# Forget-gate attention pairs: weights divided before the turn, values as 64-column stationary tiles, output written by feature

## The reference, cut to what matters

```python
s = einsum('bhqd,bhkd->bhqk', q, k) * scale + c[q] - c[k]     # c: cumulated log forget gate
p = softmax(where(causal, s, min))
fox_o = einsum('bhqk,bhkd->bhqd', p, v)                       # 8 heads x 64
diff_o = rms_norm(a1 - lam * a2, subln_g) * 0.8               # 4 heads x 128
m = concat([fox_o, diff_o]) @ w_out                           # 1024 x 1024
x = x + rms_norm(m, mix_post_g)
```

## Time and profile before

| what | value |
|---|---|
| median of 3 runs | 992.6 us |
| span of the profiled execution (first to last instruction) | 990.5 us |
| TensorE busy | 986.0 us, 100% of the span |
| VectorE, ScalarE, GpSimd busy | 711.5, 486.3, 213.1 us |
| granted TensorE clock | 1.000 |

### The profile page before, as it was taken

The page is one execution under the profiler, slowest core; times in us unless marked ns, Lnnn a source line. Parts: engine busy times, 40 slices in busy tenths (PEclk is TensorE's granted clock), DMA queues, the critical chain, the costliest instruction groups (busy, mean ns, idle before and its releaser), DMA issues.

```text
span 990.5 us, 14542 instructions
## 1 busy us (share of the span) xinstructions
PE 986.0 (100%) x5302; PEld 835.5 (84%) x5302; DVE 711.5 (72%) x849; ACT 486.3 (49%) x621; POOL 213.1 (22%) x215
## 2 busy tenths in 40 slices
PE   9999999999999999999999999999999999999998
PEld 6888888888888888888888888888888888888887
DVE  6766666775788767676777998678875767667674
ACT  6534343664666543434545444365555445334342
POOL 3313232014100232323112600060000012223230
PEclk9999999999999999999999999999999999999999
DMA  9665656745425656565745625544536456556561
GB/s 316 224 212 169 212 169 214 253 131 190 129 85 170 209 173 210 171 205 177 247 154 174 204 94 200 188 145 147 168 121 220 130 184 230 172 178 201 179 210 42
DMA packets 121017, 178.53 MB, mean 180 GB/s; under 512 B 5760, under 2 KB 82112, under 8 KB 120848
## 3 DMA queue, kind: packets, MB, share of 16 engines
q1 hardware_dynamic: 120048, 174.86, 53.8%
q0 software_dynamic: 576, 1.39, 0.5%
q10 hardware_dynamic: 352, 1.73, 0.5%
HBM read 176.88 MB, written 2.64 MB: 181 GB/s over the span
## 4 chain that ended last, share of the span: by engine, by line
PE 99%; DMA 0%; SPq 0%; ACT 0%; issue 0%; DVE 0%
PE acc L662 11%; PE acc L666 10%; PE acc L665 10%; PE tp L863 10%; PE gu L863 10%; PE gu L868 5%; PE tp L868 5%; PE tp L662 4%; PE tp L666 4%; PE tp L665 4%; PE gu L662 3%; PE gu L665 3%; PE gu L666 3%; PE acc L1143 2%; PE acc L1146 1%; PE acc L1172 1%
## 5 line engine op out<-in xcount | busy, mean ns | idle before, releaser
L2002 DVE TENSOR_TENSOR wlo<-raw,whi 128x2048 fp32r<-128x2048 f32 x140 | 325.7, 2331 | 153.9 <-ACT whi L1363 152.4
L1363 ACT ACTIVATE whi<-raw 128x2048 fp32r<-128x2048 f32 x150 | 285.7, 1908 | 70.3 <-PE acc L666 22.7
L863 PE MATMUL tp<-act_in,whi 128*128 128x512 f32 x432 | 102.9, 390 | 0.0
L863 PE MATMUL gu<-act_in,whi 128*128 128x512 f32 x432 | 102.6, 390 | 0.0
L1899 POOL TENSOR_TENSOR tmp<-tmp 128x256 f32<-128x256 f32 x54 | 39.7, 736 | 275.8 <-DVE tmp L2123 275.8
L1901 POOL TENSOR_TENSOR sil<-sil,tmp 128x256 f32<-128x256 f32 x54 | 88.8, 1644 | 33.5 <-ACT sil L1434 33.5
L863 PEld LDWEIGHTS gu<-act_in,whi 128*128 128x128 f32 x432 | 80.9, 188 | 16.6
L662 PE MATMUL acc<-whi,hT_hi 128*128 128x512 f32 x240 | 94.0, 392 | 0.0
L665 PE MATMUL acc<-wlo,hT_hi 128*128 128x512 f32 x240 | 93.7, 390 | 0.0
L666 PE MATMUL acc<-whi,hT_lo 128*128 128x512 f32 x240 | 93.4, 389 | 0.0
L863 PEld LDWEIGHTS tp<-act_in,whi 128*128 128x128 f32 x432 | 79.8, 188 | 15.7
(11 more groups left out here) (379 smaller groups left out, 1845.8 us busy)
## 6 DMA issues: line engine op xcount, KB each, us to landing
raw<-in_w_in SPq DMA_DIRECT2D x96, 512.0 KB, 4.7
raw<-in_down SPq DMA_DIRECT2D x66, 512.0 KB, 4.1
raw<-in_gate SPq DMA_DIRECT2D x64, 512.0 KB, 4.4
raw<-in_up SPq DMA_DIRECT2D x64, 512.0 KB, 4.9
raw<-in_w_out SPq DMA_DIRECT2D x16, 512.0 KB, 4.7
raw<-in_w_branch_hg SPq DMA_DIRECT2D x8, 512.0 KB, 4.3
raw<-in_w_branch_attn SPq DMA_DIRECT2D x8, 512.0 KB, 4.8
post<-in_post_gains SPq DMA_DIRECT2D x3, 512.0 KB, 6.2
```

The lines of the kernel that those rows point to most:

```text
L863: pe.matmul(banks[:, a, :], w_hi[:, i, a * P:(a + 1) * P], both, start=i == 0, stop=False)
L1363: act.activation(split_weights(k)[0], raw[:, k % RING, :], ACT.Copy).then_inc(hi_ready, 1)
L2002: dve.tensor_tensor(w_lo, raw[:, k % RING, :], w_hi.bitcast(F32), ALU.subtract).then_inc(lo_ready, 1)
```

## The change

- The weights of a fox pair are divided by their row sums in `e_sb`, in place, before they are turned (`fox_weights(p, h)` on VectorE: a reciprocal, one scaling of 128x256 and one of 128x128 for each head). `turn_weights` waits for that, head by head.
- `values(p)` takes the 64 value columns of a head as stationary operand and the turned weights as moving one (256 and 128 columns); the two heads stand in columns 0 to 63 and 64 to 127 of the array. The output comes by feature, both heads in one 128x256 place (`fox_place`).
- ScalarE rounds that place straight into the operand of `w_out` (`fox_out`), VectorE writes the rest (`output`, one instruction instead of four). Fills 2 and 3 and all that belongs to them are gone.
- In ScalarE's queue `fox_out(p)` stands between the two heads of `exps(p+1)` for p = 4 and 5. In VectorE's queue `half_lo(N_WOUT, 0)` and `normed(3)` stand ahead of `maxima(4)`; `late_maxima` is gone; `fox_weights` is put in; `maxima(7)` stays ahead of `weights_out(6)`; the second half of `N_WOUT + 1` is behind `weights_out(6)`, and the second half of `N_WOUT + 2` behind `output(7)`.
- TensorE waits for both copies of the weights before `values(p)` for every p (before, the second head's alone for p = 6 and 7), and does the differential half's last products and three tiles of the fox half ahead of its wait for `output(7)`.

```diff
@@ TensorE: turn_weights, values @@
+                if pair(p)[0] == 0:
+                    for h in range(2):
+                        pe.wait_ge(fox_normed, 2 * (p - 4) + h + 1)
+                        for n in range(3):
+                            to = (n + 1) % 3 * P
+                            mm = pe.transpose(turned[:, h, to:to + P], e_sb[:, h, n * P:(n + 1) * P], idn)
+                    mm.then_inc(pT_full, 1)
+                    return
...
-                pe.wait_ge(exp_done, p + 1)
-                for h in range(2):
-                    for n in range(3):
-                        mm = pe.transpose(turned[:, h, n * P:(n + 1) * P], e_sb[:, h, n * P:(n + 1) * P], idn)
-                mm.then_inc(pT_full, 1)
...
+                if kind == 0:
+                    at = [slice(64 * h, 64 * h + 64) for h in range(2)]
+                    v = [proj[:, t, FV + i * P:FV + (i + 1) * P] for t in range(TT)]
+                    o = fox_place(p)
+                    for h in range(2):
+                        pe.matmul(o[at[h], :], v[0][:, at[h]], pT_sb[:, h, 0:S], start=True, stop=False, skip_group_check=True)
+                    for h in range(2):
+                        mm = pe.matmul(o[at[h], P:S], v[1][:, at[h]], pT_sb[:, h, S:3 * P], start=False, stop=True,
+                                       skip_group_check=True)
+                    mm.then_inc(pv_done, 1)
+                    return
...
-                    if p in (6, 7) and h == 1:
-                        pe.wait_ge(pT_d, p + 1)
...
-                    pe.wait_ge(pT_a, p + 1)
-                    if p < 6:
-                        pe.wait_ge(pT_d, p + 1)
+                    weights_read(p)
@@ TensorE: behind the pairs @@
             half(N_WOUT + 1, 0, wout_banks(1), 1, 0, tiles=[2, 3], first_j=1)
+            half(N_WOUT + 1, 0, wout_banks(1), 1, 1, first_j=1)
+            half(N_WOUT + 2, 0, wout_banks(0), 0, 0, tiles=[0, 1, 2], first_j=1)
             pe.wait_ge(o_out, 8)
-            fills(T_WOUT, from_proj(MIX), 2, 3)
-            half(N_WOUT + 1, 0, wout_banks(1), 1, 1, first_j=1)
-            filled(T_WOUT, 3)
-            for b in range(2):
-                half(N_WOUT + 2 + b, 0, wout_banks(b), 0, 0, first_j=1).then_inc(acc_bank, 1)
-            filled(T_WOUT, 4)
+            half(N_WOUT + 2, 0, wout_banks(0), 0, 0, tiles=[3], first_j=1).then_inc(acc_bank, 1)
+            half(N_WOUT + 3, 0, wout_banks(1), 0, 0, first_j=1).then_inc(acc_bank, 1)
@@ ScalarE @@
+            def fox_out(p):
+
+                act.wait_ge(pv_done, p + 1)
+                act.activation(act_hi[:, p - 4, :], fox_place(p), ACT.Copy).then_inc(fox_hi_ready, 1)
...
-                    if p < 7:
-                        exps(p + 1)
+                    if p < 6:
+                        exps(p + 1, between=p)
+                    elif p == 6:
+                        exps(7)
+                        fox_out(6)
+                    else:
+                        fox_out(7)
@@ VectorE @@
+            def fox_weights(p, h):
+
+                n, i = 6 * (p % 2), p - 4
+                if h:
+                    dve.wait_ge(exp_done, p + 1)
+                else:
+                    dve.wait_ge(fox_exp, i + 1)
+                of_head = slice(h, h + 3, 2)
+                dve.reciprocal(rden[:, n:n + 4][:, of_head], den[:, of_head]).then_inc(rden_ready if h else fox_rden, 1)
...
+                for r, cols in enumerate((slice(0, S), slice(S, 3 * P))):
+                    e = e_sb[:, h, cols]
+                    ins = dve.tensor_scalar(e, e, rden[:, n + 2 * r + h:n + 2 * r + h + 1], None, ALU.mult)
+                ins.then_inc(fox_normed, 1)
...
+                if kind == 0:
+                    dve.wait_ge(fox_hi_ready, i + 1)
+                    dve.tensor_tensor(act_lo[:, i, :], fox_place(p), act_hi[:, i, :].bitcast(F32), ALU.subtract)\
+                       .then_inc(o_out, 1)
+                    return
...
+                half_lo(N_WOUT, 0)
+                normed(3)
                 maxima(4)
-                normed(3)
                 k_out(5)
-                half_lo(N_WOUT, 0)
                 fill_scaled(T_WOUT, 0)
                 fill_scaled(T_WOUT, 1)
+                for h in range(2):
+                    fox_weights(4, h)
                 half_lo(N_WOUT, 1)
                 block_out(N_WIN, 0, 23)
                 fill_rest(T_WOUT, 0)
                 weights_out(4)
-                late_maxima(5)
+                maxima(5)
                 k_out(6)
-                maxima(5, late_found=True)
+                fox_weights(5, 0)
                 output(4)
+                fox_weights(5, 1)
                 fill_rest(T_WOUT, 1)
                 half_lo(N_WOUT + 1, 0)
                 weights_out(5)
-                late_maxima(6)
+                maxima(6)
                 k_out(7)
-                maxima(6, late_found=True)
+                fox_weights(6, 0)
                 output(5)
-                half_lo(N_WOUT + 1, 1)
-                reciprocals(6)
+                fox_weights(6, 1)
                 maxima(7)
                 weights_out(6)
+                half_lo(N_WOUT + 1, 1)
+                for h in range(2):
+                    fox_weights(7, h)
                 output(6)
+                weights_out(7)
                 half_lo(N_WOUT + 2, 0)
-                weights_out(7)
+                output(7)
                 half_lo(N_WOUT + 2, 1)
-                output(7)
```

More of the change, by code:

```diff
@@ L62 @@
 BY_TILE, BY_HALF = [(0, 0), (0, 1), (1, 0), (1, 1)], [(0, 0), (1, 0), (0, 1), (1, 1)]
-DIFF_FIRST = [(0, 1), (1, 1), (0, 0), (1, 0)]
-FILLS = [DIFF_FIRST if u == T_WOUT else BY_HALF if u in (T_FFN1, T_WOUT2) else BY_TILE for u in range(9)]
+DIFF_ONLY = [(0, 1), (1, 1)]
+FILLS = [DIFF_ONLY if u == T_WOUT else BY_HALF if u in (T_FFN1, T_WOUT2) else BY_TILE for u in range(9)]
 C_ID, C_TRI, C_ONES, C_MASK, C_COS, C_SIN, C_SAME = 0, 128, 256, 384, 512, 528, 544
@@ L341, in o_place, with fox_place @@
         def o_place(p, h, t):
[L343 to L347, removed]
+            return gu[:, 1 - t, 0:P]
+        def fox_place(p):
+            return score_banks(p)[:, 1, S:2 * S]
         def wout_banks(b):
@@ L1026, in values @@
                     pe.wait_ge(o_out, p - 1)
+                if kind == 0:
[9 more added lines that the diff above has]
+                    return
                 for h in range(1 if kind == 1 else 2):
[L1028 to L1030 removed]
+                    col = (None, DV + i * P, AV + i * S + h * P)[kind]
+                    v = [proj[:, t, col:col + P] for t in range(TT)]
                     if kind == 2:
@@ L1534, in exps, with fox_exps @@
                     return
-                for h in range(2):
-                    lt, el = late_half(p, h), early_half(p, h)
-                    n = 4 * (p % 2)
-                    act.activation(e_sb[:, h, 0:S], lt, ACT.Exp, bias=nmx[:, n + h:n + h + 1], accum_out=den[:, h:h + 1])
-                    last = act.activation(e_sb[:, h, S:3 * P], el, ACT.Exp, bias=nmx[:, n + 2 + h:n + 3 + h],
-                                          accum_out=den[:, 2 + h:3 + h])
-                last.then_inc(exp_done, 1)
+                fox_exps(p, 0)
+                if between is not None:
+                    fox_out(between)
+                fox_exps(p, 1)
+            def fox_out(p):
+                act.wait_ge(pv_done, p + 1)
+                act.activation(act_hi[:, p - 4, :], fox_place(p), ACT.Copy).then_inc(fox_hi_ready, 1)
+            def fox_exps(p, h):
+                lt, el = late_half(p, h), early_half(p, h)
+                n = 4 * (p % 2)
+                act.activation(e_sb[:, h, 0:S], lt, ACT.Exp, bias=nmx[:, n + h:n + h + 1], accum_out=den[:, h:h + 1])
+                act.activation(e_sb[:, h, S:3 * P], el, ACT.Exp, bias=nmx[:, n + 2 + h:n + 3 + h],
+                               accum_out=den[:, 2 + h:3 + h]).then_inc(exp_done if h else fox_exp, 1)
             def weights_out(p):
@@ L1726, in _ @@
             hi(N_WOUT + 3)
-            fills(T_WOUT, 2, 3)
             hi(N_FFN2)
@@ L2211, in k_out, with maxima @@
                        .then_inc(kT_ready, 1)
-            def late_maxima(p):
-                dve.wait_ge(scores_done, p + 1)
-                n = 4 * (p % 2)
-                dve.tensor_reduce(mx[:, n:n + 2], heads(late(p), 2), AX, ALU.max)
-            def maxima(p, late_found=False):
+            def maxima(p):
                 dve.wait_ge(scores_done, p + 1)
@@ L2251, in weights_out @@
                 dve.tensor_copy(pT_sb[:, 1, :], turned[:, 1, 0:3 * P]).then_inc(pT_d, 1)
-                if pair(p)[0] == 0 and p != 6:
-                    reciprocals(p)
             def late_reciprocals(p):
```

30 lines of the change are left out of this document (12 added, 18 removed).

## The result

| | before | after |
|---|---|---|
| median of 4 runs each | 992.65 us (992.27 to 992.74) | 997.36 us (997.18 to 997.58) |
| ratio, 95% interval | | 1.0050 (1.0038 to 1.0061) |
| span of the profiled execution | 990.5 us | 995.4 us |

The kernel became 4.7 us slower. 2.2 us slower was forecast (994.8, range 992.6 to 996.0). The page of the kernel after, beside the earlier trace rows: engines, and the chain that ended last.

What follows compares the result with a forecast made beforehand. TensorE, busy 986.0 of 990.5 us, was taken to bound the kernel, so its new waits cost their full time. +1.27 + 0.88 + 0.59 + 0.3 - 0.85 = +2.2 us gave 994.8 us, range 992.6 to 996.0.

Steps and rivals of the forecast that it cites:

- Step (e): From values(7) to the first turn of x: 14.35 us instead of 15.21, the load taking 4.6; -0.85 us.
- 0.3 of the gain lost to the load: From values(7) to the first turn of x: the later load takes 0.3 us of what TensorE saves there.
- Step (a): First `w_out` product: waits for `fill_rest(0)` behind both rescaled heads of pair 4 on VectorE; +1.27 us.
- The rescalings themselves: VectorE's reciprocal and two scalings of the fox weights: 0.69 us a head, 1.38 a pair.
- Step (b): From `turn_qk(p+2)` to `scores(p+2)`, p = 4 and 5: 3.64 us instead of 3.20, shorter values lost; twice +0.44.
- (c): At values(6): TensorE now waits for both copies, with `weights_out(6)` behind `maxima(7)` on VectorE; +0.59 us.
- (d): From values(6) to values(7): VectorE's queue makes it 4.48 us instead of 4.18; +0.3 us.
- The values: TensorE's values of a pair: 1.0 us instead of 1.26, with lower end 0.78 and upper end 1.56.
- the prediction's 1.2 us by that rule: A pair's values if each change of tiling mode drains the array fully: 1.2 instead of 1.0 us.
- Smaller waits: Rival 1: a head's rescaling costs VectorE half of 0.69 us or is half covered; +0.2, 992.8 us; chance 0.23.
- Tiles that don't overlap: Rival 3: a pair's values take 1.56 us, in the open only at values(7); +2.75, 995.3 us; chance 0.15.
- Faster: Rival 2: VectorE's rescaling is covered, TensorE sets the pace, 1.9 us of work goes; 990.7 us; chance 0.08.

Runs made afterwards that it cites:

- The first experiment: The changed kernel with the second half of `lo(N_WOUT + 2)` ahead of `output(7)` in VectorE's queue; 994.76 us, ratio 1.0021.
- outputs first: The changed kernel with `fox_out(p)` and `output(p)` ahead of the next pair's exponentials and rescaling, for p = 4 and 5; 996.03 us, ratio 1.0037.
- full width: The changed kernel with all 128 value columns of the pair as stationary operand for either head, so no tiles work side by side; 998.84 us, ratio 1.0065.
- `maxima(4)` first: The changed kernel with `maxima(4)` ahead of `normed(3)` again in VectorE's queue; 997.00 us, ratio 1.0043.

## Why the prediction was wrong

The direction was right, and so were the places of all five waits. The number failed at one term.

**Step (e) failed, at "the traffic ends a quarter into the second at 301, 4.6 later".** The load's duration was carried over from the kernel before as a constant. In the kernel after it is 7.15 us, mainly because TensorE's next block of instructions is fetched while the load runs. Moved out of the load with every stretch from `scores(4)` to values(7) kept, the fetch gives 1.7 us back; moved into it, it takes 0.9 us, what of the 1.6 us isn't slack. The rest is the reading: 4.6 is where the moved bytes of a row 1 us wide seem to end, but in the kernel before itself the piece landed 5.3 us after its first issue, and with the fetch moved away in the kernel after it lands 5.4 after it. In the kernel before this didn't show, because ScalarE rounded the piece ahead of it until 302.6. 1.7 for the fetch and 0.7 for the reading, less 0.3 for the earlier issue, are the 2.15 that (e) was off, to 0.1. With it goes "0.3 of the gain lost to the load": all of the gain and 1.3 us more were lost. The first experiment, whose load has no fetch in its first 4 us and is issued earlier, runs at 994.76 us, where 994.8 was forecast; but by chance, since its load takes 5.2 us and not 4.6, and its TensorE doesn't wait at the first turn of x (13.88 where 14.35 was forecast), while (a) to (d) were longer than their terms.

**Step (a) was mis-sized, 1.58 for 1.27.** The half `lo` that was to fill idle time for nothing starts at 270.08, just ahead of GpSimd's first instruction for the norm of `normed(3)`. Beside the earlier trace rows this is GpSimd in the kernel after:

```profile
270.79 0.57 POOL L1904 TENSOR_SCALAR ms<-sums 128x2 f32<-128x2 f32 x1 [4.24 <-ACT junk L1586]
271.44 0.69 POOL L1905 TENSOR_TENSOR rstd<-ms,mhalf 128x2 f32<-128x2 f32 x1
```

The norm ends at 272.13 instead of 271.71, and `normed(3)` starts at 272.17 where 271.75 was forecast. The rescalings themselves, 0.65 us a head from start to start, are within 0.04 of the term.

**Step (b)**, 3.74 and 3.76 for 3.64, was right in its chain and 0.1 short each time. That the order of the two outputs was the cause, and that the shorter values are lost there, is shown by the runs "outputs first" and "full width".

**Steps (c) and (d)**, 3.59 for 3.53 and 4.33 for 4.48, stood.

**The values** cost 0.80 us (281.13 to 281.93), less than the 1.0 taken and next to the 0.78 of tiles always at work. The 0.15 for a first and last instruction alone and the 0.09 for going over to tiles are not seen. By the Trainium skill (TensorEngine Tiling (Array Packing), Tiling Modes, Key Properties) a change of mode drains the array; the prediction's 1.2 us by that rule is 0.4 more than the trace shows.

**The rivals.** Smaller waits fell: it had a head at half of 0.69 us and the trace has 0.65, and every wait came out as long as forecast or longer. Even with the scaling cut to 8 columns half of those of (a) and (b) remained. Tiles that don't overlap fell by 0.80. Faster fell at (b), as foreseen. No case had a load that lands over 0.5 us later, so 997.4 lay outside the range.

## What to carry to other kernels

A load's time from issue to landing is not a constant that moves with the load: where it is on the path, read what else the DMA engines do at the new time, the instruction queues too, and keep 2 us for it in the range. Take its length from the row of its last issue and the time to landing, not from where the bytes seem to end. A change in the number of instructions, even of waits that never wait, can move a fetch into such a load. And when idle time of VectorE is to be filled, look at what GpSimd does in the same microsecond, since the result waited for may be its.

## What the runs showed of the hardware

- **A fetch of instructions in a load.** One of 0.02 MB in the midst of a load of 1 MB, 0.8 to 3.4 us behind the issue of its second half, goes with a landing of that half 6.1 to 6.9 us after issue instead of 4.8 to 5.1, though it takes 0.9% of sixteen engines over 7 us, which is 1 us of one. By the Trainium skill (Runtime: NRT & Kernel Launch, Instruction fetch mechanics) the cost of going over to the next block of instructions is mostly hidden. The trace agrees for TensorE itself, which stands nowhere at a fetch here, but not for the load beside it. That the one engine left at some 20 GB/s is the one that did the fetch is inferred, and why it loses up to 2 us to 1 us of work stays open.
- **VectorE and GpSimd.** GpSimd's 128x2 instruction took 0.57 us instead of 0.19 beside one half `lo`, the one behind it 1.55 instead of 0.69 beside two. The Trainium skill (SBUF — State Buffer, Who interferes with whom) says that a VectorE instruction with two SBUF inputs contends with a GpSimd instruction that reads SBUF; `lo` has two, and the trace agrees.
- **Half a clock behind a wait.** A wait of 2.0 us or more at the first turn of x was followed by a granted clock of 0.50 for about 3 us or longer in six traces (2.0 to 5.9 us of wait), by 1.00 in three (2.0, 2.2 and 2.5). The four matmuls of the first turn took up to 1.12 us instead of 0.66. From the first turn of x to the fourth passed 8.26 us at the full clock and 1.4 to 1.6 us more at the halved one, 1.9 more behind the wait of 5.9. One kernel goes both ways from one execution to the next (`maxima(4)` first: two of four). What decides isn't shown.
